# Conditioning units of a two-layer trunk as half rows of 512 columns, and its setup in two stages of four tiles

## The reference

```python
cond = jax.nn.silu(c)
for l in range(DEPTH):
    mod = cond @ w_ada[l] + b_ada[l]                 # 1024 x 6144 weights, one row of activations
    sh1, sc1, g1, sh2, sc2, g2 = [m[:, None, :] for m in jnp.split(mod, 6, axis=-1)]
    h = _rms_norm(x, norm1_gain[l]) * (1.0 + sc1) + sh1
    proj = h @ w_in[l]
    ...
    x = x + g1 * (o @ w_out[l])
    h = _rms_norm(x, norm2_gain[l]) * (1.0 + sc2) + sh2
    x = x + g2 * _conv_glu_ffn(h, w_ffn_up[l], ffn_conv_w[l], ffn_conv_b[l], w_ffn_down[l])
return _rms_norm(x, final_gain)
```

## Time and profile before

| | |
|---|---|
| median of 3 runs | 745.94 us (745.32 to 746.12) |
| the profiled execution | 744.75 us, of which the span is 743.0 us |
| TensorE busy | 714.7 us, 96% |
| VectorE, ScalarE, GpSimd busy | 68%, 54%, 16% |
| mean granted clock of TensorE | 0.984 of full speed |
| HBM read | 155.76 MB |

### The profile page before, as it was taken

One profiled execution on the slowest core, in us unless ns is written; L12 is line 12 of the kernel. 1 busy time (PEld: TensorE's weight loads), 2 busy tenths in 40 slices (PEclk: granted clock), 3 DMA queues, 4 the chain that ended last, 5 costly groups with the idle time before them and its releaser, 6 DMA issues.

```text
span 743.0 us, 14789 instructions
## 1 busy us (share of the span) xinstructions
PE 714.7 (96%) x6129; PEld 668.8 (90%) x6129; DVE 502.7 (68%) x906; ACT 404.1 (54%) x652; POOL 118.2 (16%) x91
## 2 busy tenths in 40 slices
PE   6879999999999999999999999989999999999997
PEld 4479878789899999999998987879999999999997
DVE  1354788655589797887767368974569666666674
ACT  2347755644475655656545765664456455544543
POOL 2000101204006444555200010110400000000001
PEclk9799999999999999999999999999999999999998
DMA  9999999728277768686934787573816555555501
GB/s 281 350 296 183 353 325 311 243 71 282 100 230 261 255 219 269 208 266 223 352 119 142 248 263 226 164 234 118 280 57 227 171 184 200 184 170 177 194 28 57
DMA packets 139830, 158.35 MB, mean 213 GB/s; under 512 B 4963, under 2 KB 133108, under 8 KB 139764
## 3 DMA queue, kind: packets, MB, share of 16 engines
q1 hardware_dynamic: 139764, 157.41, 66.5%
HBM read 155.76 MB, written 1.64 MB: 212 GB/s over the span
## 4 chain that ended last, share of the span: by engine, by line
PE 82%; ACT 6%; DVE 5%; issue 3%; SPq 2%; DMA 1%; DVEq 0%; ACTq 0%
PE bank L921 23%; PE bank L922 22%; PE bank L923 22%; PE bank L935 4%; ACT work L1516 2%; ACT w_hi L1360 2%; PE bank L1247 1%; PE bank L975 1%; DVE w_lo L1623 1%; PE bank L951 1%; DMA direct<-in_w_ada 1%; SPq L718 1%; PE bank L1278 1%; PE bank L1137 1%; PE bank L1135 1%
## 5 line engine op out<-in xcount | busy, mean ns | idle before, releaser
L921 PE MATMUL bank<-act_hi,w_hi 128*128 128x256 f32 (+1 forms) x1040 | 298.1, 287 | 5.1 <-DVE act_lo L1638 4.4
L1623 DVE TENSOR_TENSOR w_lo<-raw,w_hi 128x2048 fp32r<-128x2048 f32 (+1 forms) x97 | 233.5, 2407 | 96.7 <-ACT w_hi L1360 96.6
L922 PE MATMUL bank<-act_lo,w_hi 128*128 128x256 f32 (+1 forms) x1040 | 294.2, 283 | 0.0
L923 PE MATMUL bank<-act_hi,w_lo 128*128 128x256 f32 (+1 forms) x1040 | 294.2, 283 | 0.0
L1360 ACT ACTIVATE w_hi<-raw 128x2048 fp32r<-128x2048 f32 (+1 forms) x97 | 183.0, 1888 | 144.4 <-PE bank L923 144.0
L921 PEld LDWEIGHTS bank<-act_hi,w_hi 128*128 128x128 f32 (+1 forms) x1040 | 198.6, 191 | 15.6 <-issue 14.3
L922 PEld LDWEIGHTS bank<-act_lo,w_hi 128*128 128x128 f32 (+1 forms) x1040 | 198.7, 191 | 0.1
L923 PEld LDWEIGHTS bank<-act_hi,w_lo 128*128 128x128 f32 (+1 forms) x1040 | 198.7, 191 | 0.0
L921 PE MATMUL bank<-mlp_hi,w_hi 128*128 128x256 f32 x352 | 99.9, 284 | 0.0
L922 PE MATMUL bank<-mlp_lo,w_hi 128*128 128x256 f32 x352 | 99.6, 283 | 0.0
L923 PE MATMUL bank<-mlp_hi,w_lo 128*128 128x256 f32 x352 | 99.6, 283 | 0.0
(11 more groups left out here) (203 smaller groups left out, 840.6 us busy)
## 6 DMA issues: line engine op xcount, KB each, us to landing
direct<-in_w_ada SPq DMA_DIRECT2D x48, 1024.0 KB, 9.1
raw<-in_w_ffn_up SPq DMA_DIRECT2D x44, 1024.0 KB, 5.2
raw<-in_w_in SPq DMA_DIRECT2D x22, 1024.0 KB, 6.4
raw<-in_w_ffn_down SPq DMA_DIRECT2D x22, 1024.0 KB, 5.0
raw<-in_w_out SPq DMA_DIRECT2D x8, 1024.0 KB, 5.8
bias<-toeplitz SPq DMA_DIRECT2D x4, 384.0 KB, 12.3
heads_out<-in_x SPq DMA_DIRECT2D x1, 1024.0 KB, 5.1
out<-heads_out SPq DMA_DIRECT2D x4, 256.0 KB, 2.4
```

The costliest lines, as they stand in the source:

```text
L921: pe.matmul(dst, lh, rh, start=first, stop=False, skip_group_check=check)
L922: pe.matmul(dst, lh, rl, start=False, stop=False, skip_group_check=check)
L923: return pe.matmul(dst, ll, rh, start=False, stop=last, skip_group_check=check)
L1623: nc.vector.tensor_tensor(w_lo[n % RAW][:, s], raw[n % RAW][:, s], w_hi[n % RAW][:, s].bitcast(F32), ALU.subtract).then_inc(lo_done, 1)
```

## The change

A unit of `w_ada` that TensorE multiplies is now half of the rows of 512 columns instead of all rows of 256 columns: `ada_half` makes 4 products of 512 columns where it made 8 of 256, the first half opens the bank's sum and the second closes it. In the setup D0 and D1 are the shift of tiles 0 to 3, D2 and D3 the scale of the same tiles, D4 and D5 the shift and D6 and D7 the scale of tiles 4 to 7. Two stages of four tiles take the place of four rounds of two. The loads of D1, D2 and D3 move ahead in SP's queue, D3 ahead of the tables and of the taps' vectors. The turn of the first scale set moves ahead of the table's product; the second stage's sets stand between the single tiles 0 to 3; tiles 4 to 7 of U0 and U1 now follow in the schedule.

```diff
+SETUP_COLUMNS = (0, SETUP_ADA // 2, 2, SETUP_ADA // 2 + 2)
 def pair_units(l, u):
-    return (u // 2, u // 2 + SETUP_ADA // 2) if l == 0 and u < SETUP_ADA else (u, u + 1)
+    u = SETUP_COLUMNS[u // 2] if l == 0 and u < SETUP_ADA else u
+    return (u, u + 1)
...
-        s += [("unit", 0, 6, KT), ("evac", 0), ("split_hi", 3), ("unit", 1, 6, KT), ("evac", 1), ("split_lo", 3),
+        s += [("unit", 0, 4, KT), ("evac", 0), ("split_hi", 3), ("unit", 1, 4, KT), ("evac", 1), ("split_lo", 3),
...
+                if kind == "ada" and (l, u) not in sum_no:
+                    half, c0 = u % 2, (u - u % 2) * UC
+                    sp.dma_start(slot[:, :].rearrange("p (k n) -> p k n", k=KT // 2),
+                                 w_ada[l].rearrange("(k p) n -> p k n", p=P)[:, 4 * half:4 * half + 4, c0:c0 + 2 * UC]).then_inc(
...
             load_direct(0)
+            load_direct(1)
             rows(0, V_BADA, b_ada, 48)
...
-            load_direct(1)
+            load_direct(2)
             load_unit(0, 0)
             load_unit(0, 1)
+            load_direct(3)
...
-                for i in range(2):
-                    for g in range(4):
-                        k = 4 * i + g
-                        mm = pe.matmul(pair_bank(l, u)[32 * g:32 * g + 32, half * UC:(half + 1) * UC], cond[:, k, :],
-                                       w[:, k, :], start=(i == 0), stop=(i == 1))
+                for g in range(4):
+                    mm = pe.matmul(pair_bank(l, u)[32 * g:32 * g + 32, :], cond[:, 4 * half + g, :], w[:, g, :],
+                                   start=(half == 0), stop=(half == 1), skip_group_check=True)
...
             ada_turn(0, 0)
-            ada_half(0, 2, 0, 0)
+            ada(0, 2)
+            ada_turn(0, 2)
             pe.wait_ge(table_in, 16 * 2)
...
-            ada_half(0, 2, 1, 0)
-            pe.wait_ge(vec_in, 1)
             first_units(0, 1)
-            ada_turn(0, 2)
+            ada_half(0, 4, 0, 2)
             first_units(1, 2)
-            ada_half(0, 4, 0, 2)
+            ada_half(0, 4, 1, 2)
             first_units(2, 3)
-            ada_half(0, 4, 1, 2)
-            first_units(3, 4)
             ada_turn(0, 4)
             ada_half(0, 6, 0, 4)
-            first_units(4, 5)
+            first_units(3, 4)
             ada_half(0, 6, 1, 4)
-            first_units(5, 6)
             ada_turn(0, 6)
...
-            modulated(0, 0, 0, 0, 2)
             for i in range(2):
                 split_hi(i, unit_width(i))
+            take_rows(0, 2)
+            modulated(0, 0, 0, 0, 4)
             act.wait_ge(diag_up, 1)
...
-            take_rows(0, 2)
-            modulated(0, 0, 0, 2, 4)
             take_rows(0, 4)
+            take_rows(0, 6)
             modulated(0, 0, 0, 4, 6)
-            take_rows(0, 6)
             wait_raw(act, 2)
...
-            first_mod(0)
+            take_mod(0, 0)
             for i in range(2):
                 split_lo(i, unit_width(i))
-            for k in range(1, KT // 2):
-                first_mod(k)
+            take_mod(0, 2)
+            first_modulated(0)
+            take_mod(0, 4)
+            take_mod(0, 6)
+            first_modulated(1)
```

More of the change, by code:

```diff
@@ L694, in load_direct @@
                 slot = direct[a % DSLOTS]
-                if kind == "ada":
+                if kind == "ada" and (l, u) not in sum_no:
+                    half, c0 = u % 2, (u - u % 2) * UC
+                    sp.dma_start(slot[:, :].rearrange("p (k n) -> p k n", k=KT // 2),
+                                 w_ada[l].rearrange("(k p) n -> p k n", p=P)[:, 4 * half:4 * half + 4, c0:c0 + 2 * UC]).then_inc(
+                        direct_in[a % DSLOTS], 16)
+                elif kind == "ada":
                     sp.dma_start(slot[:, :].rearrange("p (k n) -> p k n", k=KT),
@@ L760, in _ @@
                 rows_sem[1], 16)
-            for a in range(2, SETUP_ADA):
+            for a in range(4, SETUP_ADA):
                 load_direct(a)
@@ L930, in ada_half @@
                 pe.wait_ge(direct_in[a % DSLOTS], direct_value(a))
-                w = direct[a % DSLOTS][:, :].rearrange("p (k n) -> p k n", k=KT)
-                for i in range(2):
-                    for g in range(4):
-                        k = 4 * i + g
-                        mm = pe.matmul(pair_bank(l, u)[32 * g:32 * g + 32, half * UC:(half + 1) * UC], cond[:, k, :],
-                                       w[:, k, :], start=(i == 0), stop=(i == 1))
+                w = direct[a % DSLOTS][:, :].rearrange("p (k n) -> p k n", k=KT // 2)
+                for g in range(4):
+                    mm = pe.matmul(pair_bank(l, u)[32 * g:32 * g + 32, :], cond[:, 4 * half + g, :], w[:, g, :],
+                                   start=(half == 0), stop=(half == 1), skip_group_check=True)
                 mm.then_inc(direct_used, 1)
@@ L1662, in take_mod @@
                 dve.wait_ge(ada_turned, n)
-                s = slice(2 * u, 2 * u + 4)
+                c0 = 2 * pair_units(l, u)[0]
+                s = slice(c0, c0 + 4)
                 nc.vector.tensor_reduce(mod[:, l, s], pair_bank(l, u)[:, :].rearrange("p (c g r) -> p c g r", g=4, r=32)[:, :, :, 0],
@@ L1666, in take_mod, with first_modulated @@
                 dve.wait_ge(mod_ready, n)
-                nc.vector.tensor_tensor(mod[:, l, s], mod[:, l, s], vec[:, l, V_BADA + 2 * u:V_BADA + 2 * u + 4],
+                nc.vector.tensor_tensor(mod[:, l, s], mod[:, l, s], vec[:, l, V_BADA + c0:V_BADA + c0 + 4],
                                         ALU.add).then_inc(mod_done, 1)
[L1670 to L1683, removed]
+            def first_modulated(c):
+                wait_mod(4 * c + 4)
+                own(nc.vector.scalar_tensor_tensor(amp[:, 0, 4 * c:4 * c + 4], mod[:, 0, KT + 4 * c:KT + 4 * c + 4], 1.0,
+                                                   vec[:, 0, V_N1 + 4 * c:V_N1 + 4 * c + 4], ALU.add, ALU.mult))
+                modulated(0, 0, 0, 4 * c, 4 * c + 4)
             def take_columns(l, u, n):
```

## The result

The change makes the kernel slightly slower: 747.5 us as the median of 12 executions (744.97 to 749.15), against 745.28 us (743.46 to 746.37) for 12 of the kernel before beside them. The ratio is 1.0028, with a 95% interval of 1.0017 to 1.0039, so 1.3 to 2.9 us. 747.5 lies in the predicted range and 1.3 above the predicted 746.2. That sum started from 745.94; against the 745.28 measured beside it the kernel lost 2.2 us where +0.3 was forecast, and more than the 0.2% that the prediction took as its limit of telling. So the sign is that of the case given 0.21. The profiled execution had 747.64 us and a span of 745.9, at a mean granted clock of 0.977.

The account below looks back on a forecast made before the run. The prediction took TensorE's idle and half-clock time in the setup, before about 50 us, as the bound. Setup +0.5 and pairs -0.2 gave +0.3 on the median 745.94, about 746.2 us; range 743.9 to 748.2.

Parts of the forecast that it names:

- the case given 0.21: Whole kernel: measurably slower than before, by more than 0.2% or 1.5 us, above 747.4 us; chance 0.21.
- The frame: Setup: a change is worth what it takes from TensorE's idle and half-clock time before about 50 us.
- Conditioning's form in the layers: 16 pairs outside the setup: half the instructions, same columns, worth -0.2 us, bounds -0.8 and 0.
- Part 2: Setup, landing of D3: taken at 22.6 us, 23.5 if rows of 2 KB move no faster.
- If rows of 2 KB move no faster: Setup loads: without a faster transfer rate from the longer rows, D3 lands at 23.5 us.
- Part 3: Setup, TensorE through stage one: D3's product 22.6 to 24.5 us, turn at 25.3, tile 0 from 29.0 to 31.0.
- Part 4: Setup clock: rises at about 32.7 us, 3.7 after the dense run starts at 29.0; 0.9 us lost.
- Part 5: Setup, stage two: products end at 39.9 us, turn at 40.7, first act_lo of tile 4 at 43.8.
- Part 6: Setup, tiles 4 to 7: U0 ends at 46.7 us, U2 starts at 49.7; clock fall over gapped U0 costs 0.1.
- the forecast's own +0.5: Setup as a whole: the predicted net change in time, +0.5 us.
- The clock stays down longer: Rival: in the setup one more 3.4 us stretch passes at half clock, +1.7 us, 747.9 us; chance 0.20.

Follow-up runs that it names:

- experiment 1: Kernel before with only the layers' 16 conditioning pairs as half rows of 512 columns, setup untouched: 744.87 us, ratio 0.9996 to the kernel before.
- experiment 2: Changed kernel with its stages and orders, but all conditioning units as full rows of 256 columns again: 750.17 us, ratio 1.0075 to the kernel before.
- experiment 5: Changed kernel plus 24 useless products in TensorE's wait ahead of tile 4: 745.81 us, ratio 1.0018 to the kernel before.
- 7: Changed kernel plus useless products early: 12 behind D2's product, 3 behind D3's, 8 ahead of tile 0: 747.37 us, ratio 1.0034 to the kernel before.
- experiment 11: Changed kernel plus useless products: 34 behind D2's product, 6 behind D3's, 10 behind its turn: 743.18 us, ratio 0.9976 to the kernel before.
- 3: Changed kernel with ScalarE's high split of U2's front half moved ahead of its adds for tiles 4 to 7: 746.71 us, ratio 1.0026 to the kernel before.
- 8: Changed kernel with U0 and U1 multiplied by turns for each of tiles 4 to 7: 746.53 us, ratio 1.0019 to the kernel before.
- experiment 4: Changed kernel with U2's front half split early and multiplied in the wait ahead of tile 4: 742.44 us, ratio 0.9966 to the kernel before.
- 10: Kernel before, without the change, with U2's front half multiplied in its own last wait: 742.55 us, ratio 0.9966 to the kernel before.
- 12: Changed kernel with early useless products, 21 more in the wait before tile 4, and tiles 4 to 7 by turns: 741.69 us, ratio 0.9953.
- experiment 6: Kernel before plus 24 useless products in its own last wait, ahead of its tile 6: 745.14 us, ratio 1.0001 to the kernel before.
- 9: Changed kernel with U2's front half in the wait before tile 4 and U0, U1 by turns for tiles 4 to 7: 743.21 us, ratio 0.9973.

## Why the prediction came out as it did

**The frame was right.** TensorE's idle and half-clock time before 50 us decided. Conditioning's form in the layers was worth little or nothing (taken at -0.2, between -0.8 and 0; experiment 1 gives -0.3, with an interval from -1.0 to +0.4).

**Part 2** was right in the value (22.6 taken, 22.29 measured) and wrong in a bound. "If rows of 2 KB move no faster" was given 23.5; experiment 2 had D3's product at 24.54. The bound counted the transfers' rate and left out that SP was held at an issue, 3.46 us for 0.85. The change thus gained more by its rows than any sum of the prediction had in it. The Trainium skill (DMA: Bandwidth & Descriptors, Why small descriptors are slow) would have put the gain in rate at about 4%, by the estimate of part 2; the windows show 378 to 385 GB/s for 347 to 349, some 8 to 11%. Here the measurement decides.

**Part 3** came out 0.8 us early at the turn and 0.9 at tile 0. 0.3 of it is D3's landing; the rest is that D3's product began at full clock, which fell at 22.8, and took 1.50 us for the 1.93 assumed. **Part 4**: the rise was forecast at 32.7 and came at 33.0, but its working did not hold. It counted 3.7 us from the start of an unbroken run of conditioning and dense products; here that run starts at 28.19 and the rise is 4.8 us behind it, in experiment 5 it is 5.8 (27.70 to 33.5). The run's early start and the longer delay cancel, which is luck. The reading of the window from 22.5 us was wrong too: up to 24.62 it holds the product of D2 and that of the table, not transposes, so it says nothing on the sentence of the Trainium skill beside it. **Part 5**: the turn of stage two at 40.45 for 40.7, tile 4 at 43.59 for 43.8. Up to here the account was 0.2 us too high.

**Part 6 failed**, in one term: "The idle stretch before 43.8 should bring the same fall, but earlier, over the gapped tiles of U0, where it costs 0.1." The fall came, 43.3 us, and over U0 it did cost 0.1 (46.59 - 43.59 = 3.0 for 2.9). But it lasted 6.8 us instead of 3.4, over the four tiles of U1: 51.00 - 46.59 = 4.4 us for 3.0. That is +1.4. U1 had begun 0.1 early, so U2 starts at 51.00 for 49.7, and with the forecast's own +0.5 that is the setup's +1.86. It is what the rival *The clock stays down longer* describes, one more stretch of 3.4 us over dense work (1.7 us, 747.9). What was held against it, that one wait of two had not brought a fall, was about the fall; the length of the stretch was never argued.

**The rival's reason isn't shown.** It was that the gapped tiles of U0 do not hold the clock up. Of the profiled executions with these gaps and nothing in the wait, that of the kernel after and that of 7 have 6.8 us; that of 2 has 3.4 at the same distances, and that of 11 has 3.4 where the clock fell 1.3 us behind tile 4 (43.5 to 46.9). With the gaps closed 3 and 8 have 3.4, as 2 has with them. So the gaps are not enough, and whether closing them helps can't be told from one profiled execution each. What decides between 3.4 and 6.8 us stays open; that equal kernels have both is also what the two groups of executions suggest. That 747.5 lies so near to the rival's 747.9 is in part luck: in the profiled execution 1.04 us come from elsewhere, as told below.

That the clock makes the setup's loss is shown in the trace by experiment 5 (no work moved, the clock held, the mark back by 2.06). In the time of the kernel half-clock time shows clearly only in 11, where no useful work moved, and that is the stretch ahead of tile 0; 4, 10 and 12 move or reorder work as well. How much of the median's 2.2 us is the stretch behind tile 4 isn't shown, since the intervals of 5 and 8 overlap that of the kernel after. That a filled wait is worth more than the change is shown by 4 and 10 having the same ratio.

**Outside the prediction** is the 1.04 us behind the mark, most of it in the stretch from 391.4 at the boundary of the layers. Experiment 1, whose pairs have the new form, gives no loss (its profiled execution has a stretch at 537.7); the profiled executions of 4 and 6 have a stretch at 386.1 and 389.1, and 6 has the kernel before's own instructions there. So it isn't the new form that makes it. Why an execution has it, or has one at 187 and 538 as those of 5 and 11 (and one near 538 alone in 1, 2 and 9), stays open. It may account for a part of the difference between the two groups of the kernel after, and no run here separates it from the setup's stretch.

## What to carry to other kernels

When an edit concentrates several short waits of TensorE into one, ask what TensorE does in the some 7 us behind it (6.8 is the longest half-clock stretch seen there): a fall of the clock over gapped tiles costs little (0.1 us here), over dense work it costs half of each microsecond. Count with the long stretch in the sum: with the same wait and the same gaps it was 3.4 us in two profiled executions and 6.8 in two. Fill such a wait with useful products of a later unit if their operands can be ready (here 0.34% below the kernel before, in either order of the setup); products without use hold the clock too, if they cover the whole wait (0.24% in experiment 11; in 5 and 6 it showed in the trace and not in the time), and gave nothing in 7, where they ended too soon and 8 stood on the path at half clock. Judge a setup of 60 us by a mark behind it in the trace and not by the time of the kernel alone, since half-clock stretches elsewhere move single executions by 1 to 3 us; and profile more than one execution before a mark is trusted to less than 1.7 us, what half a clock costs over 3.4 us.

## What was not expected of the hardware

- Rows of 1 KB cost more than rate. The issue of a small load behind two such units held SP for 3.46 us, behind units of 2 KB rows for 0.85 (experiment 2).
- TensorE was occupied without a break from 24.55 to 33.0 us of the kernel after, the last 4.8 us with conditioning and dense products, all of it at half clock. The Trainium skill (TensorE: Matmul & The Clock Gate, Part 4) has transposes count for less than products; no run here shows it: up to 28.19 there are turns and the table's product, but the 4.8 us of products behind them were at half clock as well.
- The first fall of the clock lies at 12.5 us in the kernel after and at 14.0 in that of experiment 4, at 15.9 in the kernel before and at 13.6 in that of experiment 6, though each pair has the same instructions of TensorE up to there; and one kernel's executions differ by 0.977 to 0.984 in mean clock. A difference under some 1.5 us between two single profiles says nothing until the half-clock stretches of both are laid side by side.
